# Three gate chunks of block one by seven block products each, with the q and k norm moved behind the first

## What is computed

```python
hn = rms_norm(x, g_mix[l])
proj = hn @ w_in[l]
(qa, ka, va, ra, alr, qb, kb, vb, qi, ki, wi, gate_a, gate_b) = jnp.split(proj, split_points, axis=-1)
ya = gla_mixer(qa, ka, va, ra, alr, w_alpha2[l], b_alpha[l], g_gla[l]) @ w_br_gla[l]
qb = rms_norm(qb.reshape(b, t, ATT_HEADS, ATT_DH), g_q[l])
kb = rms_norm(kb.reshape(b, t, ATT_HEADS, ATT_DH), g_k[l])
...
yb = dsa_mixer(qb, kb, vb, qi, ki, wi, rel_bias) @ w_br_att[l]
mixed = jax.nn.sigmoid(gate_a) * ya + jax.nn.sigmoid(gate_b) * yb
x = x + mixed @ w_out[l]
x = x + hier_moe(rms_norm(x, g_ffn[l]), ...)
```

## Time and profile before

| | |
|---|---|
| median of 3 runs | 915.82 us (915.25 to 918.32) |
| span of the profiled execution | 914.7 us |
| PE busy | 770.7 us (84%) |
| VectorE busy | 302.1 us (33%) |
| ScalarE busy | 207.7 us (23%) |
| GpSimd busy | 68.8 us (8%) |
| read from HBM | 307.77 MB |

### The profile page before, as it was taken

How to read it: one execution, slowest core, us unless ns; L and a number is a source line. 1 busy time by engine, 2 the same in 40 slices (tenths; PEclk the granted TensorE clock), 3 DMA queues, 4 the chain that set the end, 5 groups by cost and what they waited for, 6 DMA issues and landing times.

```text
span 914.7 us, 22062 instructions
## 1 busy us (share of the span) xinstructions
PE 770.7 (84%) x9739; PEld 597.1 (65%) x9739; DVE 302.1 (33%) x752; ACT 207.7 (23%) x441; POOL 68.8 (8%) x76
## 2 busy tenths in 40 slices
PE   7999999999999999999998888767675676856764
PEld 4888888777777678867657666546464454644543
DVE  2676722453444375875343111101010010010101
ACT  2213332321422244436442101001020010100100
POOL 6200020000100030640000000000000000000000
PEclk9999999999999999999999999988898998897987
DMA  9996646357899999452769999999999999999995
GB/s 301 327 355 219 219 165 241 148 200 267 294 408 406 405 357 386 140 231 93 298 254 355 426 427 424 426 426 428 428 428 428 429 428 427 431 428 428 428 428 231
DMA packets 55577, 310.23 MB, mean 339 GB/s; under 512 B 5442, under 2 KB 7194, under 8 KB 43104
## 3 DMA queue, kind: packets, MB, share of 16 engines
q1 hardware_dynamic: 50720, 301.08, 82.6%
q0 software_dynamic: 2912, 4.37, 1.6%
q10 hardware_dynamic: 1888, 3.94, 1.2%
HBM read 307.77 MB, written 4.19 MB: 341 GB/s over the span
## 4 chain that ended last, share of the span: by engine, by line
PE 59%; DMA 34%; DVE 3%; issue 3%; ACT 1%; DVEq 0%; SPq 0%; ACTq 0%
PE ps L2088 56%; DMA ring<-in_w_up 25%; DMA ring<-in_w_down 5%; DMA ring<-in_w_gate 3%; PE ps L2114 1%; PE ps L2261 1%; PE ps L2451 0%; DMA xx<-in_x 0%; ACT y_high_words L1019 0%; DVE arena L1635 0%; PE ps L2128 0%; DVE ring L1577 0%; PE ps L2221 0%; PE ps L2145 0%; PE ps L2498 0%
## 5 line engine op out<-in xcount | busy, mean ns | idle before, releaser
L2088 PE MATMUL ps<-ring,arena 128*32 128x128 f32 (+3 forms) x4944 | 245.9, 319 | 90.2 <-DMA ring<-in_w_gate 43.2
L2088 PEld LDWEIGHTS ps<-ring,arena 128*32 128x32 f32 (+1 forms) x4944 | 191.7, 126 | 139.4 <-DMA ring<-in_w_gate 52.0
L2088 PE MATMUL ps<-arena 32*128 32x256 f32 (+9 forms) x1476 | 129.9, 346 | 2.5 <-issue 1.8
L2088 PEld LDWEIGHTS ps<-arena 32*128 32x128 f32 (+5 forms) x1476 | 97.7, 163 | 29.4 <-issue 21.2
L2088 PE MATMUL ps<-ring,const 128*32 128x256 f32 x864 | 59.9, 421 | 26.9 <-DMA ring<-in_w_down 23.7
L2088 PE MATMUL ps<-ring,xx 128*128 128x256 f32 (+2 forms) x312 | 80.0, 409 | 0.8 <-issue 0.6
L2088 PE MATMUL ps<-xx,ring 128*128 128x256 f32 x352 | 78.8, 382 | 0.0
L2088 PEld LDWEIGHTS ps<-xx,ring 128*128 128x128 f32 x352 | 66.1, 190 | 9.5 <-issue 0.7
L2088 PEld LDWEIGHTS ps<-ring,xx 128*128 128x128 f32 x312 | 58.5, 190 | 15.8 <-issue 6.5
L2088 PEld LDWEIGHTS ps<-ring,const 128*32 128x32 f32 x864 | 28.6, 119 | 53.8 <-issue 37.0
L1647 DVE TENSOR_TENSOR w_fa<-g_dil,ps 128x128 f32<-128x128 f32 x16 | 4.6, 288 | 135.1 <-ACT g_dil L1007 135.1
(11 more groups left out here) (348 smaller groups left out, 807.3 us busy)
## 6 DMA issues: line engine op xcount, KB each, us to landing
ring<-in_w_up SPq DMA_DIRECT2D x36, 2048.0 KB, 25.1
ring<-in_w_gate SPq DMA_DIRECT2D x35, 2048.0 KB, 23.6
ring<-in_w_down SPq DMA_DIRECT2D x33, 2048.0 KB, 23.9
ring<-in_w_in SPq DMA_DIRECT2D x15, 2048.0 KB, 21.2
arena<-in_w_down SPq DMA_DIRECT2D x5, 2048.0 KB, 8.1
ring<-in_w_out SPq DMA_DIRECT2D x4, 2048.0 KB, 8.9
arena<-in_w_gate SPq DMA_DIRECT2D x4, 2048.0 KB, 12.6
arena<-in_w_up SPq DMA_DIRECT2D x3, 2048.0 KB, 11.2
```

Of the source, the lines that this page charges most:

```text
L2088: ins = pe.matmul(dst, w, x, start=start, stop=stop, skip_group_check=True)
```

## The change

The three gate chunks go by seven products too, in the same scheme, but with the weights still stationary: a product is 2 groups of 4 matmuls, 128 features by 128 columns stationary, 128 tokens moving. The sums of `x` are the ones of the chunks before; for chunk 2 two of them are made again (their place is taken by `gate_b`). The weight sums lie in the arena where an early `w_down` of the experts goes, so SP waits for the chunks' end before it loads that. ScalarE copies five times a chunk out of PSUM into the gate tiles, VectorE adds, and the sigmoid is then taken in place. On VectorE the q and k norm moves from ahead of the states to behind chunk 0's additions. The transposes of `og` move on PE from ahead of chunk 2 into it, ahead of its product 6. The counters of the semaphores that later chunks use are shifted by what the three chunks add. The core of the diff:

```diff
+        GATE_BANKS = [(2, 0, 1), (3, 2, 0), (1, 3, 2)]
...
             load_moe1("w_up", w["w_up"][0:EG], FIRST1[1], 0)
             sp.wait_ge(s_rel_dram, 16)
+            sp.wait_ge(s_sev, gates_out(3))
+            sp.wait_ge(s_isum, gates_added(3))
             load_moe1("w_down", w["w_down"][0:EG], FIRST1[2], 0)
...
+            def gate_eviction(n, p):
...
+                act.wait_ge(s_prod, gate_done(n, p))
+                act.activation(dst, bank_pair(bz if p == 5 else bx), ACT.Copy).then_inc(s_sev, 1)
+            def gate_sigmoid(n):
...
+                act.wait_ge(s_sev, gates_out(n + 1))
+                act.wait_ge(s_isum, gates_added(n + 1))
+                act.activation(gate, gate, ACT.Sigmoid).then_inc(s_pev_a, 1)
+            for p in GATE_OUTS:
+                gate_eviction(0, p)
+            act.wait_ge(s_go, 1)
...
+            gate_eviction(1, 1)
             root(ROOTS["dsa"])
...
+            gate_sigmoid(0)
+            for p in (6, 5, 7):
+                gate_eviction(1, p)
+            root(ROOTS["gla"])
+            gate_eviction(1, 4)
+            gate_eviction(2, 1)
+            gate_sigmoid(1)
+            act.wait_ge(s_gtp, 1)
+            act.activation(gla_T, tiles4(4), ACT.Copy, scale=gcol[:, R_GLA:R_GLA + 1]).then_inc(s_gT, 1)
+            for p in (6, 5, 7, 4):
+                gate_eviction(2, p)
+            gate_sigmoid(2)
...
+            def gate_weight_sum(n, j):
...
+                if j == 1:
...
+                        dve.wait_ge(s_prod, gate_done(n - 1, 5))
...
+                out, x, y = {1: (t1, b12, b11), 2: (t2, b22, t1), 3: (b12, b22, b12), 4: (b21, b21, t2)}[j]
+                dve.tensor_tensor(out, x, y, ALU.subtract).then_inc(s_tsum, 1)
...
+            gate_weight_sum(0, 1)
             add_part(ra, 3)
             add_third(ra, 3)
...
             dve.tensor_tensor(kdec, kdec, ka, ALU.mult).then_inc(s_kdec, 1)
-            dve.wait_ge(s_pev_a, 3)
-            dve.wait_ge(s_pev_d, 3)
-            group_norm("dsa", arena[:, 0:2048], xs[:, :, :].rearrange("p a b -> p (a b)"), 32, DH).then_inc(s_hn, 1)
+            gate_weight_sum(0, 2)
+            gate_weight_sum(0, 3)
...
+            gate_second(0)
+            gate_weight_sum(0, 4)
+            for j in (1, 2, 3):
+                gate_weight_sum(1, j)
+            dve.wait_ge(s_rel_dram, 16)
+            s1, s2 = gate_x[2][0:2]
+            dve.tensor_tensor(s1, xnT[:, 0:4, P:T], xnT[:, 4:8, P:T], ALU.add).then_inc(s_asum, 1)
+            dve.wait_ge(s_asum, 4 + 1)
+            dve.tensor_tensor(s2, s1, xnT[:, 0:4, 0:P], ALU.subtract).then_inc(s_asum, 1)
+            gate_part(0)
+            gate_third(0)
...
+            group_norm("dsa", arena[:, 0:2048], xs[:, :, :].rearrange("p a b -> p (a b)"), 32, DH).then_inc(s_hn, 1)
+            gate_second(1)
+            gate_weight_sum(1, 4)
             dve.wait_ge(s_gog, 2)
...
             step(group_norm("gla", ogf, xs[:, 0, :], TT * GH, GDV))
             dve.tensor_tensor(og, og, ra, ALU.mult).then_inc(s_gn, 1)
+            for j in (1, 2, 3):
+                gate_weight_sum(2, j)
+            gate_part(1)
+            gate_third(1)
+            gate_second(2)
+            gate_weight_sum(2, 4)
+            gate_part(2)
+            gate_third(2)
             dve.wait_ge(s_bm, 2)
...
+            def gate_chunk(n, between={}):
...
+                for p in GATE_ORDER:
...
+                    if p in (3, 4, 6, 7):
+                        pe.wait_ge(s_sev, gate_out(n, {6: 1, 7: 6, 3: 5, 4: 7}[p]))
+                    if p in (4, 5, 6, 7):
+                        pe.wait_ge(s_tsum, 4 * (N7 + n) + {5: 1, 6: 2, 7: 3, 4: 4}[p])
...
+                    for m in range(2):
+                        for k in range(4):
+                            ins = mm(bank(b, P, m * P), w4[:, k, m * P:(m + 1) * P], x[:, k, :],
+                                     start and m == 0 and k == 0, False)
+                    ins.then_inc(s_prod, 1)
...
-            gate_chunk(CH_GATE + 1)
-            pe.wait_ge(s_gn, 1)
-            transposes(4, lambda m, tt: og[:, tt, m * P:(m + 1) * P], 4, s_gtp, 4)
-            gate_chunk(CH_GATE + 2)
+            gate_chunk(1)
+            gate_chunk(2, {6: gla_transposes})
             pe.wait_ge(s_hn, 1)
...
-            pe.wait_ge(s_pev_a, CH_GATE + 3)
+            pe.wait_ge(s_isum, gates_added(3))
             for t in range(8):
                 last_gate(t)
```

More of the change, by code:

```diff
@@ L198, in program @@
         a_sum = [[kb3(at + 2 * i, 4, P) for i in range(4)] for at in (50, 82)]
+        gate_t = [kb3(80 + 4 * i, 4, T) for i in range(2)]
+        gate_c22 = [kb3(at, 2, P) for at in (88, 89, 88)]
+        gate_x = [a_sum[0], a_sum[0], [kb3(76, 4, P), kb3(78, 4, P)] + a_sum[0][2:]]
         q2r = xs[:, 0, :].rearrange("p (t n) -> p t n", t=TT)
@@ L298, in program @@
         s_relu = sem("index_relu")
-        s_isum = sem("index_summed")
+        s_isum = sem("index_summed_then_gate_products_added")
         s_mask = sem("selection_mask_then_weights_of_first_slots")
@@ L441, in program, with gates_out, gates_added @@
         ORDER2 = [(j, kind) for j in range(EG) for kind in "gud"]
+        N_GATE7 = 3
+        def gates_out(n):
+            return 4 * N7 + 1 + 5 * n
+        def gates_added(n):
+            return TT + 3 * n
         def turn_value(eng, s, q, per=RING):
@@ L1116, in _ @@
             act.activation(ra, ra, ACT.Silu).then_inc(s_pev_a, 1)
-            root(ROOTS["dsa"])
[L1118 to L1131, removed]
+            def gate_eviction(n, p):
+                bx, _, bz = GATE_BANKS[n]
+                dst = {1: gate_quarter(n, 0, 0), 6: gate_quarter(n, 0, 1), 5: gate_c22[n],
+                       7: gate_quarter(n, 1, 1), 4: gate_quarter(n, 1, 0)}[p]
+                act.wait_ge(s_prod, gate_done(n, p))
+                act.activation(dst, bank_pair(bz if p == 5 else bx), ACT.Copy).then_inc(s_sev, 1)
@@ new lines, in gate_sigmoid @@
+            def gate_sigmoid(n):
+                gate = (gate_a, gate_b)[n // 2][:, 4 * (n % 2):4 * (n % 2) + 4, :]
+                act.wait_ge(s_sev, gates_out(n + 1))
[4 more added lines that the diff above has]
+            act.wait_ge(s_go, 1)
+            for i in range(2):
+                act.activation(og.rearrange("p t (n i e) -> p t n i e", n=2, i=2)[:, :, :, i],
+                               bank(6 + i).rearrange("p (t n e) -> p t n e", t=TT, n=2),
+                               ACT.Copy).then_inc(s_gog, 1)
@@ L1589, in x_sum @@
                 if j in (2, 4):
-                    dve.wait_ge(s_asum, 4 * block + j // 2)
+                    dve.wait_ge(s_asum, (4 + 2) * block + j // 2)
                 x, y, op = {1: (a21, a22, ALU.add), 2: (sums[0], a11, ALU.subtract), 3: (a11, a21, ALU.subtract),
@@ L2761, in gate_chunk, with gla_transposes @@
                 read[0] += 1
+            def gla_transposes():
+                pe.wait_ge(s_gn, 1)
+                transposes(4, lambda m, tt: og[:, tt, m * P:(m + 1) * P], 4, s_gtp, 4)
             pe.wait_ge(s_kdec, 1)
@@ L2774, in _ @@
             evicted(6, 7)
-            gate_chunk(CH_GATE)
+            gate_chunk(0)
             pe.wait_ge(s_st, 1)
```

106 lines of the change are left out of this document (85 added, 21 removed).

## The result

| | before | after |
|---|---|---|
| median of 4 runs | 915.54 us (915.14 to 918.32) | 930.61 us (928.84 to 931.91) |
| span of the profiled execution | 914.7 us | 930.1 us |
| chunk 0 to last gate chunk | 45.44 us | 52.49 us |
| PE busy in 97 to 146 us | 49.00 us | 43.74 us |

The ratio is 1.0154 with a 95% interval of 1.0129 to 1.0179: 15.1 us where +6.6 was forecast, outside the range. The loss has two parts, and only one of them lies where the kernel was changed.

What follows compares the result with a forecast made beforehand. PE was taken to bound the changed stage. Waits of +5.3 us and a slow clock of +1.3 us made +6.6 us on a median of 915.82: 922.4 us, range 914.0 to 925.0.

Steps and rivals of the forecast that it cites:

- The rate of a record: Gate chunks on PE: 0.115 us a record, 12.95 us a chunk, saving 3.2 us over three if no product waits.
- load and matmul overlap: Gate products on PE: weight loads run during matmuls; taken in turn, a chunk would be 25 us.
- The gated output: VectorE's output norm and product with ra: og ready at 131.75 us, 7 us later than before.
- The meeting of mask and sums: Chunk 2: GpSimd's mask additions and VectorE's weight sums run one behind the other, costing 6.9 us, until 142.25.
- Product six waited: Chunk 2 on PE: product six waits from 133.5 to 136.5 us for the second weight sum.
- The last gate chunk: End of the gate stage: start at 152.7 instead of 147.35 us, +5.3; with +1.3 for the clock, +6.6.
- passes one to one: From the gate stage to the kernel's end: PE's shift at 147.35 us reaches the end at full size.
- Rivals A to D: A: mask, sums pass, 914.3, 0.16; B: no waits, 912.6, 0.04; C: delay absorbed, 917 to 920, 0.08; D: serial loads, 949, 0.01.
- ScalarE's table load for the sigmoid: Chunk 2: sigmoid 1.02, gla_T copy 1.11, eviction 0.38 us, ended at 145.4, so product seven waits 5.2 us.
- the slow stretch behind the first wait: Chunk 2, PE clock: a slow stretch here vanishes in the second wait and costs nothing.
- that behind the second: Chunk 2, PE clock: a slow stretch after product seven's wait costs 0 to 1.7 us, 3.4 if longer; +1.3 taken.
- rival E: More clock loss, or a further wait in chunk 1 where ScalarE has 0.3 us to spare: above 925 us, chance 0.05.

Runs made afterwards that it cites:

- experiment 3: The changed kernel with GpSimd's two mask additions put behind the third weight sum of chunk two: 921.73 us (914.81 to 928.06).
- experiment 2: The changed kernel with twenty more one-column matmuls (80 TensorE instructions) ahead of the second experts' loop: 923.43 us, ratio 1.0076.
- 1: The kernel before with eleven more one-column matmuls (44 TensorE instructions) ahead of the second experts' loop: 921.15 us, ratio 1.0047.
- experiment 12: The kernel before with sixteen more one-column matmuls (64 TensorE instructions) ahead of the second experts' loop, run again: median 922.5 us (915.5 to 926.5).
- 4: The changed kernel with VectorE's two additions of chunk one ahead of chunk two's three weight sums, the meeting with GpSimd kept: 932.42 us.
- before + 104: The kernel before with 26 more one-column matmuls (104 TensorE instructions) ahead of the second experts' loop: 915.6 us (913.6 to 921.0).
- + 140: The kernel before with 35 more one-column matmuls (140 TensorE instructions) ahead of the second experts' loop: 916.0 us (914.4 to 918.0).
- experiment 8: The changed kernel with 80 instructions ahead of the loop, mask additions behind the fourth weight sum, q/k norm behind chunk two's sums: 913.95 us, ratio 0.9982.
- experiment 11: As experiment 8, with the mask additions behind chunk 0's last addition and chunk two's fourth weight sum moved into VectorE's wait: 916.46 us, ratio 1.0013.

## Why the prediction fell short

**Right, and shown.** The rate of a record came out at 12.70/112 = 0.113 us (0.115 was taken from the earlier trace rows). That load and matmul overlap holds for all three chunks. The gated output came at 132.4; less the 1.06 us by which the stage began late that is 131.4, and 131.75 was forecast. The meeting of mask and sums went as the earlier trace rows had it: both ran one behind the other, 132.33 to 142.29 us for work of 3.6 + 6.9, and without it (experiment 3) the stage takes 44.61 us, less than before's 45.44. Product six waited 2.96 us (3.0 forecast). The last gate chunk came 7.05 us late against the stage's start, and +6.6 was forecast. That this passes one to one holds to 740 us: 7.36 us. With the loop moved (experiment 2) the kernel takes 923.4 us, 1 us from the forecast. Rivals A to D are out.

**Sized a little wrong.** ScalarE's table load for the sigmoid (1.28 us) was counted as done ahead of the wait; it came behind it, at 143.04. It would have put product seven 1.3 us later than forecast, but the sums ended 1.0 us earlier (142.29 - 1.06 = 141.2 against 142.25); that the two nearly cancel is luck. On the clock, the slow stretch behind the first wait vanished in the second, as said, and that behind the second cost 5.37 - 3.74 = 1.6 us (1.3 taken); in experiment 2 it cost 6.58 - 3.74 = 2.8 us.

**Wrong: the step that passes the stage's shift to the end and adds nothing on the way.** The sum had no term for TensorE's program. The chunks add 298 instructions, 144 matmuls and 144 loads among them, and move everything behind them; the loop's jump back went, by the count above, from 36 ahead of a packet's edge to 6 behind one, and in three of five returns the loop was fetched again: +8.0 us, 7.2 by experiment 2. The catch-all rival E ("more clock, or a further wait in chunk 1") had the side right and the cause wrong. The page of before had a hint that I didn't follow: the instruction queue carried just as many packets as the program has, though the loop ran six times, so it was held whole, and what is held can be lost.

**How 27 packets cost 8 us** is only partly settled. TensorE's stall is 4.89 us at the jump and 2.5 and 1.2 later, but the loop is bound by DMA, and transfers are issued 24 us ahead of their landing, 4.9 us apart; from 739.80 to 862.13 DMA moves 425 and 424 GB/s, much as in the passes before, 429 and 428. The end of the weight stream shows where the time is. Busy tenths and GB/s of DMA in slices of 0.7 us, in before from 880 us, then in after from 895 us:

```profile
DMA  9999998999999899999989999998764521100000
GB/s 421 421 398 492 421 468 374 421 421 398 492 445 445 374 421 421 398 492 445 445 374 421 421 421 468 445 445 374 328 281 187 234 117 70 47 0 0 0 0 0
```

```profile
DMA  8998999999899999998986454445443211100000
GB/s 375 538 445 375 445 398 398 492 445 421 374 398 445 398 515 445 398 398 374 445 375 281 211 234 187 211 211 211 211 187 140 94 70 47 47 23 0 0 0 23
```

In after DMA's busy share falls to about half at 910 us, 10 us before the last transfer lands; in before the tail is some 5 us. In most profiles the tail grows with the packets: some 5 us in 2 (47), 7 in 3 (56), 8 in 1 (64) and 10 in 12 (73); but in 4 (74) it is only some 6. It looks as if some engines lag behind the others. My reading is that the instruction packets are dealt to a few engines, that one of 16 KB at an engine's share of 428 GB/s costs it 0.6 us, and that a 2 MB transfer lands with its slowest part: 13 of 27 on the worst engine would make the 8 us. The record doesn't name a packet's engine, so this is argued, not shown.

**Open.** Which returns miss. Near an edge it changes from execution to execution of one program (experiment 12). Eight packets against seven would fit, if the cut lies as said above. A request for the packet behind the loop that crosses the jump would fit most rows too: where returns miss, one packet fewer has come by the end of the first pass (45 in before + 44 and + 64, 46 in after) than where the loop is moved further (46 in before + 104 and + 140, 47 in after + 80); but before has 45 as well, and its profile has no miss. Nor was it looked into why a few of before's own 92 runs lie above 920 us.

## What to carry to other kernels

A change of instruction counts on an engine also moves every loop behind it: compare the packets of the instruction queue and the time per pass before blaming the stage, and try a few idle instructions ahead of the loop. Before a two-input sum goes to VectorE, look at what GpSimd does in that stretch: ordering the two by a semaphore gave back all 7 us of the stage. And where each engine works strictly in turn, put what releases the bottleneck engine ahead of what only its successor needs: experiment 8's stage is the shortest, 42.30 us, though in the total no gain is shown.

## What the hardware showed

- TensorE held a loop of 1,620 instructions over five jumps without a fetch, and lost it in others of the same length: 9 packets of 16 KB and 0.9 to 4.2 us in each pass that misses.
- A stall of 4.9 us on TensorE behind the jump (740.04): the last one-column matmul of a pass at 739.80, the first matmul of the next at 744.93.
- GpSimd's additions hold up even a VectorE operation with one small SBUF input: 3.13 us in place of 0.18 (experiment 11). The Trainium skill, "SBUF — State Buffer", section "Who interferes with whom", says so of sums with two SBUF inputs, with which the runs agree, and of a scalar operation in its two-port mode; in which mode this one ran, no run shows.
- After waits of 2.96 and 3.02 us TensorE ran at 0.54 and 0.70 of full clock for the next 32 records; after 0.93 and 1.65 us (experiment 3), but also after 2.95 us (experiment 2), the same records ran at full speed.
